# Mixture-of-experts units of 32 token slots on four column quarters of the array, with a deeper pipeline

## The chip, the cores and the metric

The kernel runs on one core of a Trainium2 chip. The metric is the device time of one execution in microseconds (us), taken as the median of several runs. A core has TensorE (PE, with PEld for its weight loads), VectorE (DVE), ScalarE (ACT), GpSimd (POOL) and SyncE (SP), 16 DMA engines that all queues share, SBUF of 128 partitions, and PSUM in 8 banks of 128 x 512 floats. Everything here is float32 unless said otherwise.

## What is computed

The reference is two layers of a hybrid trunk over 1024 tokens of width 1024. Each layer is a mixer (stick-breaking attention in layer 0, a convolution module in layer 1) followed by a mixture of experts, and the change touches only the latter:

```
idx, wts = route(hf, w_router, b_router)          # 2 of 16 experts for each token
xb = h_pad[row_tok].reshape(n_blk, EXPERT_BLOCK, D)
def expert_block(args):
    xe, e = args
    return (jax.nn.silu(xe @ w_gate[e]) * (xe @ w_up[e])) @ w_down[e]
...
y = jnp.zeros((T + 1, D), yb.dtype).at[row_tok].add(yb * row_w[:, None].astype(yb.dtype))
```

With D = 1024 and an inner width of 512, an expert has 1024 x 512 weights for gate, as many for up, and 512 x 1024 for down: 2 MB each, 6 MB in all, so 96 MB for a layer. The 2048 (token, expert) pairs of a layer fall unevenly on the experts. For the inputs of the reference the counts are 92, 109, 113, 218, 178, 178, 143, 145, 60, 133, 138, 119, 128, 133, 68, 93 in the first layer and 29, 35, 36, 24, 187, 48, 108, 187, 148, 95, 369, 284, 130, 139, 75, 154 in the second.

## The kernel before

The program is written per engine, with semaphores between the engines. For each layer, `moe(l)` on each engine does the following.

**Routing.** DVE picks the two experts of each token, PE sums the counts, and DVE turns them into `bounds` (for each expert, the number of its first unit) and `dest` (the slot of each pair). A unit is 64 slots of one expert (`UNIT`, L32). An expert gets as many units as its count needs and at least one: 40 units in the first layer and 40 in the second. Two products of one-hot tables (L1377, L1378; the tables are made in L1025 to L1032) give `slot_tok` (L1036), a table with a column for each unit that tells which row of the DRAM tensor `h_rows` each partition is to fetch. With 64 slots and 128 partitions, partition p < 64 fetches the first half (512 columns) of slot p's row and partition 64 + p the second half.

**Gather (POOL, L459 to L461).** POOL copies the unit's column of the table to `idx_now`, drains, and issues an indirect DMA of 128 rows of 2 KB to `xg`. There is one `xg`. After each gather, POOL waits for the unit's output, stores it (L474, two DMAs of 64 rows x 2 KB to `expert_rows`), and then waits until the gather has landed and the stores too, before it goes on.

**Products (PE).** For a unit b, PE multiplies the turned rows `xT` with gate and up (L1417). `xT[:, c, :]` is the stationary operand: 128 rows of the contraction by 64 slots, so it fills half of the array's columns. Two products run at a time, one for each column half (`UNIT * t`), and each half makes its own half of the inner width. A part of 256 columns holds 128 of gate and 128 of up. For each part f of two, 16 products of 256 columns fill bank f. Then PE turns the first half of `ha` (L1406), turns the next unit's gathered rows (L1386, four transposes), does the first quarter of down (L1399), turns the second half of `ha`, and does the rest of down. Down for a unit is 8 products of 512 columns, again on two column halves.

**Between them.** ACT applies silu to each part (L644) and scales half of the next unit's turned rows (L634, four activations of 128 x 64). DVE multiplies silu with up (L1064), scales the other half (L1053), copies the turned `ha` (L1069) and multiplies the unit's output by the modulation gate (L1073, 128 x 512).

**Weights (SP, L316 to L326).** Two sets of three 2 MB buffers hold the weights of an even and of an odd expert. When the last unit of expert i has done gate and up, SP issues the gate and up weights of expert i + 2 (L323), and when its down is done, the down weights (L326).

**After the units.** For each tile of 128 tokens POOL gathers the two expert rows of each token (L483), and DVE adds them to `xq` with the router's weights (L1078, L1080).

The order of the work around the change is written out by hand. Each engine has a loop over the units (or over experts and their units, on PE), and the semaphores count units.

## Time and profile before

| | |
|---|---|
| median of 3 runs | 2388.29 us (2388.24 to 2390.66) |
| the profiled execution, its own time | 2393.53 us |
| span of the profiled execution | 2391.9 us |
| granted TensorE clock, mean | 0.946 of 2.4 GHz |
| PE busy | 2167.1 us, 91% of the span |
| DVE, ACT, POOL busy | 48%, 31%, 11% |
| DMA | 391.49 MB, mean 164 GB/s |
| gate and up products (L1417) | 5120 matmul instructions, 571.9 us busy |
| down products (L1399) | 1280 matmul instructions, 311.3 us busy |

The profile is one execution of the program. A float32 product is two matmul instructions in it, a transpose is one. Busy time of PE includes its pipelining, so the distance from one start to the next tells more than the duration of one instruction. "issue" as a cause of idle time means that nothing that the profile shows was waited for. For a DMA the time to landing is from its issue to the last of its 16 semaphore updates.

### The profile page before, as it was taken

Reading aid. Unit: us, or ns where it says so; the run is one execution under the profiler, and the core shown is the slowest. Engines: PE = TensorE matmul, PEld = TensorE weight load, DVE = VectorE, ACT = ScalarE, POOL = GpSimd, SP = SyncE. Lnnn points to the kernel's source line nnn. Section 1 sums busy time; section 2 is a strip of 40 time slices with the busy share of each in tenths; the row PEclk is TensorE's granted clock in tenths of the full one; section 3 lists DMA queues with packets and bytes.
Section 4 is the critical chain, followed back from the end, with each engine's and each line's share of the span. In section 5 each row is a group of like instructions: output and inputs, shape, how many; then the busy total and the mean of one; then the engine's idle time right before and its main releaser. Section 6 shows DMA issues by size and latency. Waiting matters only on the chain.

```text
span 2391.9 us, 33087 instructions
## 1 busy us (share of the span) xinstructions
PE 2167.1 (91%) x12218; PEld 1202.3 (50%) x12219; DVE 1155.4 (48%) x2059; ACT 743.6 (31%) x1571; POOL 273.3 (11%) x465
## 2 busy tenths in 40 slices
PE   6999999999999399999998599989984899999991
PEld 2444444456666355555554367655443455555551
DVE  2355500678997622222222699999845122222225
ACT  3111100567775222222222411026252222222222
POOL 0000010000000112111112300000000111112113
PEclk8999999899999699999999699999986999999996
DMA  9166410003301665566666400300025777624646
GB/s 390 72 246 246 176 54 0 36 19 150 150 10 52 266 247 187 222 256 254 254 254 254 158 36 35 140 36 1 0 97 202 310 322 286 261 86 154 246 153 224
DMA packets 51578, 391.49 MB, mean 164 GB/s; under 512 B 9009, under 2 KB 9265, under 8 KB 33841
## 3 DMA queue, kind: packets, MB, share of 16 engines
q1 hardware_dynamic: 22514, 298.12, 30.9%
q0 software_dynamic: 28992, 92.40, 11.4%
q8 instruction: 46, 0.75, 0.1%
q14 instruction: 26, 0.21, 0.0%
HBM read 340.12 MB, written 50.37 MB: 163 GB/s over the span
## 4 chain that ended last, share of the span: by engine, by line
PE 77%; DVE 13%; DMA 5%; issue 2%; ACT 2%; POOL 0%; POOLq 0%; SPq 0%; DVEq 0%
PE ps L1417 21%; PE ps L1399 12%; PE ps L1265 9%; DVE kv L1134 8%; PE ps L1513 5%; PE ps L1283 5%; PE ps L1339 4%; PE ps L1297 3%; PE ps L1310 3%; PE ps L1322 3%; PE ps L1481 3%; DMA expert_rows<-hT 3%; PE ps L1406 2%; PE ps L1386 1%; DMA hT<-h_rows,idx_now 1%
## 5 line engine op out<-in xcount | busy, mean ns | idle before, releaser
L1134 DVE SCALAR_TENSOR_TENSOR kv<-kv,cols 128x640 f32<-128x640 f32 (+1 forms) x390 | 305.1, 782 | 13.3
L1417 PE MATMUL ps<-kv,hT 128*64 128x256 f32 x2624 | 290.9, 379 | 0.9 <-DMA kv<-in_w_gate_up 0.9
L1417 PE MATMUL ps<-ring,hT 128*64 128x256 f32 x2496 | 281.0, 384 | 10.8 <-issue 5.1
L644 ACT ACTIVATE hT<-ps 128x128 f32<-128x128 f32 x160 | 44.4, 277 | 679.8 <-PE ps L1417 679.8
L1417 PEld LDWEIGHTS ps<-kv,hT 128*64 128x64 f32 x2624 | 201.3, 137 | 101.4 <-issue 26.4
L1417 PEld LDWEIGHTS ps<-ring,hT 128*64 128x64 f32 x2496 | 193.2, 139 | 110.4 <-issue 39.7
L1453 PE MATMUL ps<-hT,ring 128*128 128x320 f32 (+1 forms) x768 | 225.4, 455 | 6.3 <-ACT hT L525 6.3
L1265 PE MATMUL ps<-hT,ring 128*128 128x512 f32 x512 | 226.5, 601 | 1.6 <-ACT hT L525 1.6
L904 DVE TENSOR_TENSOR_SCAN pbuf<-hT 128x128 f32<-128x128 f32 (+7 forms) x128 | 173.3, 1354 | 47.6 <-ACT hT L576 47.3
L1453 PEld LDWEIGHTS ps<-hT,ring 128*128 128x128 f32 x768 | 147.2, 193 | 81.1 <-ACT hT L525 7.0
L1069 DVE COPY hT<-ps 128x128 f32<-128x128 f32 x160 | 46.7, 292 | 267.3 <-PE ps L1406 267.3
L1064 DVE TENSOR_TENSOR hT<-hT,ps 128x128 f32<-128x128 f32 x160 | 45.2, 283 | 265.0 <-ACT hT L644 265.0
L1265 PEld LDWEIGHTS ps<-hT,ring 128*128 128x128 f32 x512 | 98.9, 194 | 125.9 <-issue 123.1
L1399 PE MATMUL ps<-kv,hT 128*64 128x512 f32 x656 | 158.8, 603 | 0.0
L1399 PE MATMUL ps<-ring,hT 128*64 128x512 f32 x624 | 152.5, 608 | 0.0
L1073 DVE TENSOR_TENSOR hT<-ps,bcC 128x512 f32<-128x512 f32 x80 | 55.3, 692 | 196.6 <-PE ps L1399 196.6
L634 ACT ACTIVATE hT<-ps,modc 128x64 f32<-128x64 f32 x328 | 105.7, 402 | 85.2 <-PE ps L1386 85.2
L1513 PE MATMUL ps<-ring,hT 128*128 128x512 f32 x256 | 119.4, 624 | 9.7 <-DVE kv L1148 5.8
L576 ACT ACTIVATE hT<-ps 128x128 f32<-128x128 f32 (+7 forms) x128 | 84.7, 661 | 94.8 <-PE ps L1300 89.0
L1283 PE MATMUL ps<-ring,hT 128*128 128x512 f32 x256 | 110.0, 592 | 0.0
L891 DVE SCALAR_TENSOR_TENSOR pbuf<-kv,cond,pbuf 128x512 f32<-128x512 f32 x140 | 105.3, 752 | 5.0
L474 POOL DMA_DIRECT2D expert_rows<-hT x160 | 86.0, 538 | 179.7 <-DVE hT L1073 172.9
(240 smaller groups left out, 2475.5 us busy)
## 6 DMA issues: line engine op xcount, KB each, us to landing
ring<-in_w_gate_up SPq DMA_DIRECT2D x32, 2048.0 KB, 12.5
kv<-in_w_gate_up SPq DMA_DIRECT2D x32, 2048.0 KB, 13.1
kv<-in_w_ada SPq DMA_DIRECT2D x20, 2048.0 KB, 7.6
ring<-in_w_down SPq DMA_DIRECT2D x16, 2048.0 KB, 13.9
kv<-in_w_down SPq DMA_DIRECT2D x16, 2048.0 KB
expert_rows<-hT POOLq DMA_DIRECT2D x160, 128.0 KB, 2.5
expert_rows<-ring POOLq DMA_DIRECT2D x2, 8192.0 KB, 24.7
ring<-in_w_in SPq DMA_DIRECT2D x8, 2048.0 KB, 8.1
```

The costliest lines, as they stand in the source:

```text
L474: pool.dma_start(y_dram[l][ds(b * UNIT, UNIT), 512 * h:512 * h + 512], yo[UNIT * h:UNIT * h + UNIT, :]).then_inc(stored[l], 16)
L634: ins = nc.scalar.activation(xT[:, c, :], bank(4)[:, P * j + UNIT * h:P * j + UNIT * h + UNIT], ACT.Identity, bias=modc[:, 2 * l + 1, 0, c ...
L891: ins = V.scalar_tensor_tensor(ada_sum[:, u, :], vslot[u][:, 512 * c:512 * c + 512], cond[:, c:c + 1], ada_sum[:, u, :] if c else bias[:, ...
L904: V.tensor_tensor_scan(pbuf[:, u, D - w:D][:, ::-1], omega[:, u, 0:w][:, ::-1], omega[:, u, 0:w], 1.0, ALU.mult, ALU.bypass).then_inc(scan ...
L1134: ins = V.scalar_tensor_tensor(new, old, w_dw_c[:, c, k:k + 1], new, ALU.mult, ALU.add)
L1265: ins = mm(bank(qk_bank(cc) + half), ring[:, j % 3, 512 * c + P * q:512 * c + P * q + P], hT[:, c, 512 * half:512 * half + 512], start=(c ...
L1283: ins = mm(bank(qk_bank(t) + half), hT[:, c, t * P:(t + 1) * P], ring[:, (4 + half) % 3, 512 * c:512 * c + 512], start=(c == 0), stop=(c = ...
L1339: ins = mm(wo_bank(qb, half), oTs[qb % 2][:, c, :], ring[:, half, 512 * c:512 * c + 512], start=(c == 0), stop=(c == DC - 1))
L1399: ins = mm(bank(6)[UNIT * t:UNIT * t + UNIT, :], haT[:, f, j, :], wd[:, D * (2 * j + f) + 512 * t:D * (2 * j + f) + 512 * t + 512], start= ...
L1417: ins = mm(bank(f)[UNIT * t:UNIT * t + UNIT, 0:2 * P], xT[:, c, :], wset[s][t][:, 512 * c + 256 * f:512 * c + 256 * f + 256], start=(c == ...
L1453: ins = mm(bank((gates_bank, values_bank)[part](i) + b)[:, 0:w], ring[:, j % 3, 512 * k + P * (c % 4):512 * k + P * (c % 4) + P], hT[:, k, ...
L1513: ins = mm(out_bank(t, half), hT[:, c, t * P:(t + 1) * P], ring[:, (8 + half) % 3, 512 * c:512 * c + 512], start=(c == 0), stop=(c == DC - 1))
```

## The change

`UNIT` becomes 32 and an expert gets at least two units (`MINBLK`). Counted from the inputs as above, that makes 71 units in the first layer and 73 in the second. The 128 partitions now fetch four quarters (256 columns, 1 KB) of 32 slots' rows. The stationary operand is 128 rows by 32 slots, and four products run at a time, one for each column quarter of the array: gate and up of a unit are 8 x 4 products of 256 columns into one bank, down is 4 x 4 products of 256 columns. A unit needs two transposes for its rows and one for `ha`.

On PE the order of a step is now gate and up of unit b, the transposes of the rows of unit b + 1, down of unit b - 1, and the transpose of `ha` of unit b. The first unit of each expert stands ahead of the loop over the rest, because its down half belongs to the expert before. POOL only gathers: two gathers are in flight in two halves of `xg`, and POOL copies a landed one to `xs` (128 x 256), from which PE turns it. The drains are gone. The stores have gone to ACT: four DMAs of 32 rows x 1 KB for each unit (`store`), from one of two buffers of `yo_all`. Before it issues the stores of unit b + 1, ACT waits for those of unit b to have landed. The table has 96 columns instead of 50, and two small DVE steps make the number of pairs of units.

```diff
-UNIT = 64
-MAXBLK = (2 * T + E * (UNIT - 1)) // UNIT + 1
-TABLE = MAXBLK + 2
+UNIT = 32
+QUARTERS = P // UNIT
+MINBLK = 2
+MAXBLK = 2 * T // UNIT + MINBLK * (E - 2)
+TABLE = MAXBLK + 4
+QUARTER = D // QUARTERS
...
# gpsimd, moe
-                with pool.Fori(0, blocks) as b:
-                    pool.wait_ge(x_turned2[l], b + 2)
-                    gather(b + 2)
-                    pool.wait_ge(y_kept[l], b + 2)
-                    for h in range(2):
-                        pool.dma_start(y_dram[l][ds(b * UNIT, UNIT), 512 * h:512 * h + 512],
-                                       yo[UNIT * h:UNIT * h + UNIT, :]).then_inc(stored[l], 16)
-                    pool.wait_ge(x_gathered[l], 16 * b + 48)
-                    pool.wait_ge(stored[l], 32 * b + 48)
+                with pool.Fori(0, pairs) as i:
+                    for u in (1, 0):
+                        n = 2 * i + 2 - u
+                        pool.wait_ge(x_gathered[l][u], 16 * i + 32 - 16 * u)
+                        pool.wait_ge(x_turned2[l], n)
+                        nc.gpsimd.tensor_copy(idx_now[:, u:u + 1], slot_tok[:, ds(n + 2, 1)])
+                        nc.gpsimd.tensor_copy(xs, xg[u]).then_inc(x_ready[l], 1)
+                        pool.wait_ge(table_made[l], 1)
+                        pool.wait_ge(x_ready[l], n)
+                        gather(u)
+                pool.wait_ge(rows_stored[l], 1)
...
# scalar, moe
+                def store(b, half):
+                    act.wait_ge(y_kept[l], b + 2)
+                    for q in range(QUARTERS):
+                        act.dma_start(y_dram[l][ds(b * UNIT, UNIT), QUARTER * q:QUARTER * (q + 1)],
+                                      yo_all[UNIT * q:UNIT * (q + 1), ds(half * QUARTER, QUARTER)]
+                                      ).then_inc(y_stored[l], 16)
...
+                silu(0)
+                keep(1)
+                silu(1)
+                keep(2)
+                store(0, 0)
+                with act.Fori(0, blocks - 2) as b:
+                    silu(b + 2)
+                    keep(b + 3)
+                    act.wait_ge(y_stored[l], 16 * QUARTERS * b + 16 * QUARTERS)
+                    store(b + 1, (b + 1) & 1)
...
+                store(blocks - 1, (blocks + 1) & 1)
+                act.wait_ge(y_stored[l], 16 * QUARTERS * blocks)
+                nc.scalar.activation(table_ahead[:, l:l + 1], eps[:, :], ACT.Sqrt).then_inc(rows_stored[l], 1)
...
# vector, moe: the loop over the units
+                with dve.Fori(0, blocks - 3) as b:
+                    gated_half(b + 3)
+                    keep(b + 4)
+                    keep_y(b + 2, b & 1)
+                    keep_ha(b + 3)
+                    dve.wait_ge(y_stored[l], 16 * QUARTERS * b + 32 * QUARTERS)
...
# tensor, moe
+                def gate_up(b, s):
+                    pe.wait_ge(xT_kept[l], b + 1)
+                    pe.wait_ge(xT_kept2[l], b + 1)
+                    for c in range(DC):
+                        for q in range(QUARTERS):
+                            ins = mm(bank(0)[UNIT * q:UNIT * (q + 1), 0:2 * P], xT[:, c, :],
+                                     wset[s][q // 2][:, 512 * c + 256 * (q % 2):512 * c + 256 * (q % 2) + 256],
+                                     start=(c == 0), stop=(c == DC - 1), skip_group_check=True)
+                    ins.then_inc(up_done[l], 1)
...
+                    with pe.Fori(first + 1, end) as b:
+                        gate_up(b, s)
+                        pe.wait_ge(x_ready[l], b + 1)
+                        turn_rows()
+                        pe.wait_ge(w_loaded[s][2], 16 * (E // 2) * l + 16 + 16 * i)
+                        down(b - 1, s)
+                        turn_ha(b)
```

How the instructions stand, on PE in the loop over the units of an expert. Before, `ps<-ring,hT 64x256` is gate and up, `64x512` is down, and `ps<-ident,hT` are transposes:

```order
L1412 ISA [waits xT_kept20,xT_kept0]
L1417 MATMUL ps<-ring,hT 64x256 [waits w_loaded001,w_loaded000]
L1417 MATMUL ps<-ring,hT 64x256 x31
L1405 ISA
L1406 MATMUL ps<-ident,hT 128x128 [waits ha_made0]
L1383 ISA
L1386 MATMUL ps<-ident,hT 128x128 [waits x_gathered0]
L1386 MATMUL ps<-ident,hT 128x128 x3
L1399 MATMUL ps<-ring,hT 64x512 [waits y_kept0,haT_kept0,w_loaded002]
L1399 MATMUL ps<-ring,hT 64x512
L1405 REGISTER_ALU
L1406 MATMUL ps<-ident,hT 128x128 [waits ha_made0]
```

The same loop in the changed kernel (L1446 gate and up, L1438 the rows, L1460 down, L1453 `ha`):

```order
L1446 MATMUL ps<-ring,hT 32x256 [waits xT_kept20,xT_kept0]
L1446 MATMUL ps<-ring,hT 32x256 x31
L1438 MATMUL ps<-ident,hT 128x128 [waits x_ready0]
L1438 MATMUL ps<-ident,hT 128x128
L1460 MATMUL ps<-ring,hT 32x256 [waits y_kept0,haT_kept0,w_loaded02]
L1460 MATMUL ps<-ring,hT 32x256 x15
L1453 MATMUL ps<-ident,hT 128x128 [waits ha_made0]
L1481 REGISTER_ALU
L1481 COMPARE_AND_BRANCH
```

The six down products that stood behind the second transpose of `ha` are gone from there, and all of down now stands between the transposes of two different units.

On ACT, the loop over the units before (from its first branch on):

```order
L641 UNCONDITIONAL_BRANCH
L641 ISA
L644 ACT_TABLE_LOAD
L644 ACTIVATE hT<-ps 128x128 [waits up_done0]
L643 REGISTER_ALU
L644 ACTIVATE hT<-ps 128x128 [waits up_done0]
L630 REGISTER_ALU
L634 ACTIVATE hT<-ps,modc 128x64 [waits x_turned0]
L634 ACTIVATE hT<-ps,modc 128x64 x3
L641 REGISTER_ALU
L641 COMPARE_AND_BRANCH
```

And in the changed kernel (`expert_rows<-hT` are the stores):

```order
L670 UNCONDITIONAL_BRANCH
L670 ISA
L654 ACTIVATE hT<-ps 128x128 [waits up_done0]
L644 REGISTER_ALU
L647 ACTIVATE hT<-ps,modc 128x32 [waits x_turned0]
L647 ACTIVATE hT<-ps,modc 128x32 x3
L673 ISA
L659 ISA [waits y_kept0,y_stored0]
L659 REGISTER_ALU
L659 ISA
L659 DMA expert_rows<-hT 32x256
L659 ISA
```

The table load has left the loop (it stands once, ahead of it), and four DMAs with two waits have come in behind the activations; the other three DMAs follow with an `ISA` ahead of each.

## Rows read from the trace of the kernel before

**Rows 1.** The page, busy time of each engine.
```profile
PE 2167.1 (91%) x12218; PEld 1202.3 (50%) x12219; DVE 1155.4 (48%) x2059; ACT 743.6 (31%) x1571; POOL 273.3 (11%) x465
```
**Rows 2.** The page, the chain that ended last, shares by engine.
```profile
PE 77%; DVE 13%; DMA 5%; issue 2%; ACT 2%; POOL 0%; POOLq 0%; SPq 0%; DVEq 0%
```
**Rows 3.** Windows over the units of each layer: PE, PEld, DVE, ACT, POOL, clock.
```profile
833.70:1308.50 474.80, 471.48 (x3440) 264.22 (x3440) 111.82 (x359) 124.50 (x280) 90.06 (x159) 0.99 0.63 243
1860.80:2343.80 483.00, 472.30 (x3440) 263.82 (x3440) 111.94 (x359) 124.50 (x280) 90.22 (x159) 0.99 0.58 226
```
**Rows 4.** Timeline of PE over one unit: start, us, instruction, count, idle before.
```profile
1001.30 7.08 PE L1417 MATMUL ps<-kv,hT 128*64 128x256 f32 x64
1008.31 0.33 PE L1406 MATMUL ps<-ident,hT 128*128 128x128 f32 x1
1008.48 0.60 PE L1386 MATMUL ps<-ident,hT 128*128 128x128 f32 x4
1009.07 1.08 PE L1399 MATMUL ps<-kv,hT 128*64 128x512 f32 x4
1010.08 0.33 PE L1406 MATMUL ps<-ident,hT 128*128 128x128 f32 x1
1010.34 2.79 PE L1399 MATMUL ps<-kv,hT 128*64 128x512 f32 x12
1012.97 7.08 PE L1417 MATMUL ps<-kv,hT 128*64 128x256 f32 x64
```
**Rows 5.** Line L1236 (router scores on four quarters), 790 to 795: ns min/median/max, first and last start.
```profile
L1236 PE MATMUL ps<-hT,wr x64: 272/273/297, 790.9 to 792.6; 128*32 128x128 f32 x64
```
**Rows 6.** Timelines of ACT and DVE at that unit's end.
```profile
1008.42 0.28 ACT L644 ACTIVATE hT<-ps 128x128 f32<-128x128 f32 x1 [3.18 <-PE ps L1417]
1008.89 1.29 ACT L634 ACTIVATE hT<-ps,modc 128x64 f32<-128x64 f32 x4 [0.19 <-PE ps L1386]
1010.20 1.28 ACT L644 ACT_TABLE_LOAD   x1
...
1001.52 0.69 DVE L1073 TENSOR_TENSOR hT<-ps,bcC 128x512 f32<-128x512 f32 x1 [2.44 <-PE ps L1399]
...
1009.11 1.10 DVE L1053 TENSOR_SCALAR hT<-ps,modc 128x64 f32<-128x64 f32 x4
```
**Rows 7.** Timelines of SP and POOL around a load of one expert's weights.
```profile
855.58 0.93 SPq L323 DMA_DIRECT2D ring<-in_w_gate_up  x2
860.34 0.33 SPq L326 DMA_DIRECT2D ring<-in_w_down  x1
...
857.50 1.02 POOL L461 DMA_INDIRECT hT<-h_rows,idx_now  x1 [1.06 <-issue]
861.55 1.12 POOL L474 DMA_DIRECT2D expert_rows<-hT  x2 [3.04 <-DVE hT L1073]
870.94 0.18 POOL L459 COPY idx_now<-slot_tok 128x1 int32 x1 [8.27 <-DMA expert_rows<-hT]
```
**Rows 8.** Window over that load: the last two are the DMA engines' share and GB/s.
```profile
857.00:873.00 16.00, 16.00 (x114) 8.99 (x114) 4.01 (x12) 4.60 (x9) 3.10 (x5) 1.00 0.97 407
```
**Rows 9.** Landing of that gather, of its unit's stores, of stores without a load (897 to 900).
```profile
DMA to landing us min/median/max: 9.0/9.0/9.0
...
DMA to landing us min/median/max: 7.1/7.7/8.3
...
DMA to landing us min/median/max: 2.2/2.3/2.5
```
**Rows 10.** Timeline of PE, second layer: third to fifth expert, with idle before.
```profile
1886.32 7.13 PE L1417 MATMUL ps<-ring,hT 128*64 128x256 f32 x64 [0.47 <-issue]
...
1900.72 7.13 PE L1417 MATMUL ps<-kv,hT 128*64 128x256 f32 x64 [0.94 <-DMA kv<-in_w_gate_up]
...
1916.68 7.13 PE L1417 MATMUL ps<-ring,hT 128*64 128x256 f32 x64 [2.62 <-DMA ring<-in_w_gate_up]
```
**Rows 11.** Timeline of PE, first unit of the first layer.
```profile
833.73 10.00 PE L1417 MATMUL ps<-ring,hT 128*64 128x256 f32 x64 [1.56 <-DVE hT L1053]
```
**Rows 12.** Timeline of DVE, making the table.
```profile
822.14 0.98 DVE L1027 TENSOR_TENSOR hT<-lane,kv 128x800 bf16<-128x800 f32 x1
823.16 0.43 DVE L1030 TENSOR_SCALAR hT<-hT,tokid 128x800 bf16<-128x800 bf16 x1
823.51 1.05 DVE L1032 TENSOR_TENSOR hT<-hT,tile_first 128x400 bf16<-128x400 bf16 x2
```
**Rows 13.** Timeline of POOL, start of the second layer's gathers and end of the first layer.
```profile
1854.77 1.01 POOL L461 DMA_INDIRECT hT<-h_rows,idx_now  x1 [4.04 <-issue]
...
1310.29 1.12 POOL L474 DMA_DIRECT2D expert_rows<-hT  x2 [2.90 <-DVE hT L1073]
1314.24 1.00 POOL L483 DMA_INDIRECT kv<-expert_rows,dest  x1 [2.83 <-DMA expert_rows<-hT]
```

More of the change, by code:

```diff
@@ new lines, in gather @@
+                        in_offset=bass.IndirectOffsetOnAxis(ap=idx_now[:, u:u + 1], axis=0)).then_inc(x_gathered[l][u], 16)
+                for u in range(2):
+                    nc.gpsimd.tensor_copy(idx_now[:, u:u + 1], slot_tok[:, u:u + 1]).then_inc(idx_made[l], 1)
+                    pool.wait_ge(idx_made[l], u + 2)
+                    gather(u)
+                pairs = pool.value_load(bounds[0:1, E + 1:E + 2], min_val=1, max_val=(MAXBLK + 1) // 2)
+                pool.wait_ge(x_gathered[l][0], 16)
@@ L637, in keep @@
-                    ins.then_inc(xT_kept[l], 1)
-                keep(0)
-                blocks = act.value_load(bounds[0:1, E:E + 1], min_val=1, max_val=MAXBLK)
-                with act.Fori(0, blocks) as b:
-                    for f in range(2):
-                        act.wait_ge(up_done[l], 2 * b + f + 1)
-                        nc.scalar.activation(sg[:, P * f:P * f + P], bank(f)[:, 0:P], ACT.Silu).then_inc(silu_done[l], 1)
-                    keep(b + 1)
+                    for q in range(QUARTERS):
+                        c = 2 * q
+                        ins = nc.scalar.activation(xT[:, c, :], bank(4)[:, UNIT * q:UNIT * (q + 1)],
+                                                   ACT.Identity, bias=modc[:, 2 * l + 1, 0, c:c + 1],
+                                                   scale=modc[:, 2 * l + 1, 1, c:c + 1])
@@ new lines, in keep, with silu @@
+                    ins.then_inc(xT_kept[l], 1)
+                def silu(b):
+                    act.wait_ge(up_done[l], b + 1)
+                    nc.scalar.activation(sg, bank(0)[:, 0:P], ACT.Silu).then_inc(silu_done[l], 1)
+                def store(b, half):
+                    act.wait_ge(y_kept[l], b + 2)
+                    for q in range(QUARTERS):
+                        act.dma_start(y_dram[l][ds(b * UNIT, UNIT), QUARTER * q:QUARTER * (q + 1)],
+                                      yo_all[UNIT * q:UNIT * (q + 1), ds(half * QUARTER, QUARTER)]
+                                      ).then_inc(y_stored[l], 16)
@@ new lines, in moe @@
+                keep(0)
+                dve.wait_ge(gate_loaded, 80 * (l + 1))
+                blocks = dve.value_load(bounds[0:1, E:E + 1], min_val=MINBLK * E, max_val=MAXBLK)
+                gated_half(0)
+                keep(1)
+                keep_ha(0)
+                for b in (1, 2):
+                    gated_half(b)
+                    keep(b + 1)
+                    keep_y(b - 1, (b + 1) % 2)
+                    keep_ha(b)
+                dve.wait_ge(y_stored[l], 16 * QUARTERS)
@@ new lines, in turn_ha, with down @@
+                def turn_ha(b):
+                    pe.wait_ge(ha_made[l], b + 1)
+                    nc.tensor.transpose(bank(2)[:, 0:P], ha, ident[:, :]).then_inc(ha_turned[l], 1)
+                def down(b, s):
+                    pe.wait_ge(haT_kept[l], b + 1)
+                    pe.wait_ge(y_kept[l], b + 1)
+                    for f in range(QUARTERS):
+                        for q in range(QUARTERS):
+                            ins = mm(bank(6)[UNIT * q:UNIT * (q + 1), 0:QUARTER], haT[:, UNIT * f:UNIT * (f + 1)],
+                                     wset[s][2][:, D * f + QUARTER * q:D * f + QUARTER * (q + 1)],
+                                     start=(f == 0), stop=(f == QUARTERS - 1), skip_group_check=True)
+                    ins.then_inc(down_done[l], 1)
@@ new lines, in expert @@
+                def expert(i, s, very_first=False):
+                    first = pe.value_load(bounds[0:1, ds(2 * i + s, 1)], min_val=0, max_val=MAXBLK)
+                    end = pe.value_load(bounds[0:1, ds(2 * i + s + 1, 1)], min_val=MINBLK, max_val=MAXBLK)
+                    for k in range(2):
+                        pe.wait_ge(w_loaded[s][k], 16 * (E // 2) * l + 16 + 16 * i)
+                    if very_first:
+                        gate_up(0, s)
+                        pe.wait_ge(x_ready[l], 1)
+                        turn_rows()
+                        turn_ha(0)
+                    else:
+                        gate_up(first, s)
+                        pe.wait_ge(x_ready[l], first + 1)
+                        turn_rows()
+                        down(first - 1, 1 - s)
+                        turn_ha(first)
+                    with pe.Fori(first + 1, end) as b:
+                        gate_up(b, s)
+                        pe.wait_ge(x_ready[l], b + 1)
+                        turn_rows()
+                        pe.wait_ge(w_loaded[s][2], 16 * (E // 2) * l + 16 + 16 * i)
+                        down(b - 1, s)
+                        turn_ha(b)
@@ L1433, in _ @@
+                pe.wait_ge(idx_made[l], 4)
+                turn_rows()
+                expert(0, 0, very_first=True)
+                expert(0, 1)
+                with pe.Fori(1, E // 2) as i:
+                    for s in range(2):
+                        expert(i, s)
+                last = pe.value_load(bounds[0:1, E:E + 1], min_val=MINBLK * E, max_val=MAXBLK)
+                down(last - 1, 1)
             for t in range(TT - 2):
```

197 lines of the change are left out of this document (78 added, 119 removed).

## The prediction

> **What bounds the kernel now.** I read four views. First the page: PE is busy for 91% of the span, more than twice as much as DVE, the next engine [rows 1], and the chain that ended last runs over PE for 77% [rows 2]. Then the windows over the units: the two layers' units take 474.8 + 483.0 = 957.8 us of the 2391.9, and in both PE leaves only 3 and 11 us idle while DVE and ACT are busy for a quarter of the time [rows 3]. All that the change touches in earnest lies in these windows. Third, the timeline of PE over one unit: from one unit's first product to the next one's it is 11.67 us, with no gap anywhere [rows 4]. So a unit costs what PE needs for it, and 80 units (40 and 40) explain 80 x 11.67 = 933.6 of the 957.8 us. Last, the DMA rows: a load of one expert's 6 MB occupies the queues for some 16 us at a 0.97 share [rows 8], and everything issued meanwhile lands late [rows 9]. Behind PE that costs little now; the reader should keep it in mind.
>
> **The step of 32 slots on PE.** Per slot nothing is saved in the products; what is saved is padding. The units go from 80 of 64 slots (5120) to 71 + 73 = 144 of 32 (4608), 10% less. The cost of a unit comes out of one timeline [rows 4]. From the first product of gate and up to the first transpose it is 7.01 us for 16 pairs, from down's first product to the next transpose 1.01 us for one pair of twice the width. Both fit 0.427 us for 256 columns and 0.16 to 0.18 us for each change to or from transposes. Four transposes take 0.59 us, one takes 0.26, so two 0.37. The new unit:
> - gate and up, 8 groups of four: 8 x 0.427 + 0.18 = 3.59
> - two transposes of rows: 0.37
> - down, 4 groups of four: 4 x 0.427 + 0.16 = 1.87
> - one transpose of `ha`: 0.26
>
> That is 6.09 us, and 144 x 6.09 = 877 us.
>
> This rests on four quarters really running together. The trace has that case: the router's scores put 32 products of 128 columns on four quarters, and their 64 instructions start within 1.7 us [rows 5], 0.21 us for each group of four, just half of the 0.427 for half the width. The new gate and up issue 64 instructions in 3.4 us, so at half that pace.
>
> What the windows hold besides (24 us now) stays nearly: the step from one pass over two experts to the next, 0.5 us some 15 times, 8 us; the lower clock of the first unit, whose gate and up take 10.0 instead of 7.08 us [rows 11], 4 us over both layers; the wait for weights in the second layer. There the first four experts have one unit each, now two. Their compute goes from 11.7 to 12.2 us each, both under the 16 us of a load, so the fifth expert starts where it does, at 1916.7 [rows 10]; that is 55.8 us after the first, and 55.8 - 4 x 12.2 = 7 us of waits remain. New is the end: down of the last unit cannot overlap another gate and up, 2.3 us a layer, 4.6. Sum: 877 + 8 + 4 + 7 + 4.6 = 901 us, against 957.8: **57 us less**.
>
> **Gathers.** POOL now spends a copy of 0.18 us and an issue of 1.0 us [rows 7], and the new copy of 128 x 256, which I put at 0.3 to 1 us (DVE takes 0.69 for 128 x 512 [rows 6]; POOL at half that rate is my upper end). At most 3 us in each 6.1, so covered. A gather is issued some 15 us before its transposes; the slow one took 9.0 us [rows 9]. Covered too, and if it weren't, PE would wait at the first transpose. Without the drain, which holds the second layer's first gather for 4.04 us [rows 13], that layer starts 3 us sooner.
>
> **The table.** 96 columns instead of 50: the four operations took 0.98 + 0.43 + 1.05 us for 50 [rows 12], so about 2.2 us more, plus two small steps of 0.2. On the path, twice: +5 us.
>
> **The end of a layer.** Stores to first expert-row gather is 3.95 us now [rows 13]. ACT issues four DMAs instead of two; SP's issues of this kind are 0.59 us apart (two end 0.93 after the first began, one takes 0.33 [rows 7]). So the last goes out 1.8 us after the first and lands 2.2 later [rows 9], 4.0, and a square root with its table load (1.28 [rows 6]) stands behind: +1.5 us a layer, +3.
>
> So far: -57 - 3 + 5 + 3 = **-52 us**.
>
> **The stores on ACT, the term that decides.** Put 0 at the end of a unit's gate and up stream. Silu starts at 0.3 and the four activations end by 2.0 [rows 4, 6]. Down ends at 0.18 + 0.37 + 1.71 = 2.26, DVE's product for 128 x 256 takes about 0.43 (0.69 for 512 columns [rows 6]) and starts 0.3 after, so ACT can issue its stores at 3.2. Four at 0.59 are done at 5.5, the branch at 5.7; the next silu is due at 6.4. The table load of 1.28 us that closed each unit [rows 6] is no longer in the loop; with it, ACT would be late every time. So 0.7 us are spare on ACT, and PE still has 0.4 before it needs `xT`: **1.1 us** in all.
>
> Behind the wait for the last unit's stores, ACT has its next stores and then the next silu queued, and DVE and PE follow that. If the stores take L us to land, ACT can issue no more often than every L us. Without a load L is 2.2 + 1.8 = 4.0, under 6.09: nothing. Within a load, the trace has one related case [rows 7, 9]: the gather landed at 857.50 + 9.0 = 866.5, the second of the two stores queued behind it at 862.1 + 8.3 = 870.4. Two transfers thus took 3.9 us. The same rows in four transfers: at best 3.9 plus the 1.8 us of issuing, 5.7; at worst each costs 1.95 us as before and the first still needs its 2.2, 10.0. I take 7.0, nearer the lower end, since each transfer has half as many rows. A load of 16 us takes in two such stores. They come 0.9 + 0.9 us late, less 1.1 spare: 0.7 us for each of the 28 loads that run beside units, **+20 us**. At L = 5.7 it is 0; at 8.3 the first is 2.2 late and the second, which the end of the load helps, 0.9: 2.0 each, +56; at 10 about 4.3 each, +120.
>
> Sum: -52 + 20 = -32 us. The profiled execution took 2393.5 us (span 2391.9), 5.2 above the median of 2388.3; against the median that is **2356 us**, 1.3% less.
>
> **Rivals.**
> *Stores land within the period.* L is 6.4 or less and ACT is never late: 2388.3 - 52 = 2336 us. For it: without a load they land in 2.2 to 2.5 us [rows 9]. Against it: 7 to 8 us for two within one.
>
> *Stores late, slower than before.* The place is ACT's wait for landed stores. From L = 8.1 or so each load costs over 1.9 us, 28 loads eat the 52, and the kernel is slower. At L = 9: 2.9 + 1.2 - 1.1 = 3.0 us x 28 = 84, 2420 us. For it: each small transfer has an end of its own to be waited for, four instead of two, and POOL's gathers are in flight beside. Against it: half the rows in each, and a queue that no gather stands ahead in. The Trainium skill (DMA: Bandwidth & Descriptors, Queues, rings and completion order) says that each DMA engine goes round its queues packet by packet, so a short transfer waits for a weight packet at every turn. By that rule the number of turns counts, not bytes, which speaks for this rival; rows 9 agree as far as they go.
>
> *A wait I don't see.* The step is 0.3 us longer than 6.09, from four semaphores a unit or DVE's order (scaling, then the output product): 144 x 0.3 = 43 us, 2399 us. Against it: none of these waits shows in the present unit [rows 4].
>
> *The instructions don't come fast enough.* If they came only at the present pace, 64 in 6.83 us, gate and up and down would take twice as long and the kernel over 3000 us. Rows 5 speak against it: 27 ns per instruction, where 53 are needed. The Trainium skill (TensorE: Matmul & The Clock Gate, the section on the gap of 56 ns) knows a decoding in software at about 62 ns for each matmul instruction. By that figure a unit would be some 0.8 us longer, an estimate of 120 us more. The pace in rows 5 is quicker than that rule allows, so it hardly counts here.
>
> **How the numbers follow.** Forecast (stalls of 8 to 45 us, 2344 to 2381): 0.50. Stores hidden: 0.18. Stores late: 0.22. Unseen wait: 0.07. Instruction pace: 0.03. A measurement of this kernel can tell 0.2% (4.8 us) from no change. Faster by more than that: 0.68. Of the rest 0.06 fall within it, where the late stores just eat the gain, and 0.26 are slower. The range reaches from 4 us below the hidden case (a small sum of my roundings) to the middle of the late case: 2332 to 2415 us; what lies beyond is under 0.2.
>
> **What would show it.** PE's distance from unit to unit should be 6.1 us outside loads. The router's stage should grow by 2 to 3 us. Silu's idle time should end with gate and up; where ACT's stores wait for `expert_rows` and PE's products then wait for `xT`, within loads alone, that is the +20. The forecast is wrong if the distance outside loads is over 6.3, or if the stores in a load take over 8 us or under 6 us.

## The result and the profile after

The changed kernel takes 2516.97 us in the median of its runs (2509.2 to 2524.0), the kernel before 2388.26 in the same session. The ratio is 1.0537, with a 95% interval of 1.0515 to 1.0558: **5.4% slower** where I had forecast 1.3% faster. It lies outside the range too, on the side of the rival *stores late, slower than before*, and 97 us above the time which I gave that rival.

The page of the changed kernel, against [rows 1, 2]: busy time, and the chain that ended last by engine and by line.
```profile
PE 2167.3 (86%) x19590; PEld 1192.4 (47%) x19591; DVE 1188.7 (47%) x2351; ACT 699.0 (28%) x1735; POOL 316.2 (13%) x595
...
PE 62%; DVE 14%; DMA 13%; ACTq 4%; issue 4%; ACT 2%; POOL 0%; DVEq 0%; SPq 0%; POOLq 0%
PE ps L1446 15%; DMA expert_rows<-hT 12%; PE ps L1319 9%; DVE kv L1188 7%; PE ps L1460 6%; PE ps L1579 5%; PE ps L1337 4%; PE ps L1393 4%; ACTq L659 4%; PE ps L1351 3%; PE ps L1364 3%; PE ps L1376 3%; PE ps L1547 2%; PE ps L1438 1%; PE ps L
```
PE is busy for the same 2167 us, but its share fell from 91 to 86%. What is new in the chain is a transfer, the stores of the experts' rows: 12% of it is their landing and 4% their issue on ACT. A store has no reader before the end of a layer, so a chain that runs over it runs over a wait for its buffer.

The windows over the units of both layers, against [rows 3] (busy time of PE, PEld, DVE, ACT, POOL; then granted clock, DMA share, GB/s):
```profile
833.40:1367.90 534.50, 464.48 (x7029) 255.97 (x7029) 125.23 (x496) 100.90 (x356) 107.57 (x214) 0.93 0.55 212
...
1921.20:2474.40 553.20, 479.44 (x7227) 260.28 (x7227) 128.60 (x510) 103.63 (x366) 110.54 (x220) 0.93 0.52 194
```
The units now take 534.5 + 553.2 = 1087.7 us, 130 more than before, and that is the whole loss: the stretch between the layers takes 553.3 us, before 552.3. PE idles for 70 and 74 us instead of 3 and 11, and the granted clock was 0.93 instead of 0.99.

The timeline around one load of weights shows how (start, us, engine, line, operation, count, idle time before and what ended it). L1446 is gate and up, L1460 down, L1453 the transpose of `ha`, L654 silu, L659 the stores.
```profile
853.36 1.96 ACTq L659 DMA_DIRECT2D expert_rows<-hT  x4
856.35 0.44 PE L1438 MATMUL ps<-ident,hT 128*128 128x128 f32 x2
856.47 0.28 ACT L654 ACTIVATE hT<-ps 128x128 f32<-128x128 f32 x1 [4.87 <-PE ps L1446]
...
858.84 3.66 PE L1446 MATMUL ps<-kv,hT 128*32 128x256 f32 x64
...
862.43 0.44 PE L1438 MATMUL ps<-ident,hT 128*128 128x128 f32 x2
862.80 1.93 PE L1460 MATMUL ps<-kv,hT 128*32 128x256 f32 x32
...
866.47 2.68 ACTq L659 DMA_DIRECT2D expert_rows<-hT  x4
869.48 0.28 ACT L654 ACTIVATE hT<-ps 128x128 f32<-128x128 f32 x1 [11.58 <-DMA expert_rows<-hT]
...
870.14 0.48 PE L1453 MATMUL ps<-ident,hT 128*128 128x128 f32 x1 [5.41 <-DVE hT L1098]
...
871.11 5.20 PE L1446 MATMUL ps<-kv,hT 128*32 128x256 f32 x64 [0.49 <-DVE hT L1091]
...
878.73 3.66 PE L1446 MATMUL ps<-kv,hT 128*32 128x256 f32 x64
```
The stores issued from 853.36 us hold ACT until they have landed, 12.8 us later; the next four go out at 866.47 and take 2.68 us to issue; only then comes the silu that was due at 862.6. It is 6.9 us late, and DVE and PE follow. Behind the stall gate and up take 5.20 instead of 3.66 us. The windows over the gate and up ahead of the stall and behind it (the granted clock is the figure before the last two) show why:
```profile
858.84:862.43 3.59, 3.59 (x65) 1.98 (x65) 0.62 (x2) 0.00 (x0) 0.40 (x1) 1.00 1.00 417
871.11:876.30 5.19, 5.19 (x65) 2.79 (x66) 0.38 (x2) 0.00 (x0) 0.00 (x0) 0.69 0.10 25
```
PE had been idle for 5.9 us but for one transpose, and the granted clock behind that is 0.69 instead of 1.00. The distance from 858.84 to 871.11 is 12.27 instead of 6.08 us, the next one 7.62.

The waits between the start and the end of the units, in total, times, longest:
```profile
ACT hT L654 <- DMA expert_rows<-hT: 189.8, 21, 12.0
ACT hT L654 <- issue: 161.7, 18, 10.7
...
PE ps L1453 <- DVE hT L1098: 102.8, 34, 5.8
```
ACT's waits in these rows are not all losses, since ACT is idle in every step. PE's are: 34 waits of some 3 us for the product behind a late silu.

Over all units (from the starts of L1446 in groups of 64 in the trace) the distances add up to 199.5 us above 6.083 each, and 56.9 us of these are gate and up that took longer than usual.

### The profile page after: what moved, and what is told of

Read it like the earlier page. It is cut to its first block, busy times and chain, and to the rows that moved or that the text cites. A ratio compares the mean times of both kernels' runs of the same rounds, so it can differ in the third digit from the quotient of the medians.

```text
span 2521.3 us, 51133 instructions
## 1 busy us (share of the span) xinstructions
PE 2167.3 (86%) x19590; PEld 1192.4 (47%) x19591; DVE 1188.7 (47%) x2351; ACT 699.0 (28%) x1735; POOL 316.2 (13%) x595
## 4 chain that ended last, share of the span: by engine, by line
PE 62%; DVE 14%; DMA 13%; ACTq 4%; issue 4%; ACT 2%; POOL 0%; DVEq 0%; SPq 0%; POOLq 0%
PE ps L1446 15%; DMA expert_rows<-hT 12%; PE ps L1319 9%; DVE kv L1188 7%; PE ps L1460 6%; PE ps L1579 5%; PE ps L1337 4%; PE ps L1393 4%; ACTq L659 4%; PE ps L1351 3%; PE ps L1364 3%; PE ps L1376 3%; PE ps L1547 2%; PE ps L1438 1%; PE ps L1266 1%
## 5 line engine op out<-in xcount | busy, mean ns | idle before, releaser
L1446 PE MATMUL ps<-ring,hT 128*32 128x256 f32 x4544 | 291.3, 413 | 27.8 <-issue 15.4
L1446 PE MATMUL ps<-kv,hT 128*32 128x256 f32 x4672 | 292.8, 407 | 13.8 <-DVE hT L1091 7.1
L654 ACT ACTIVATE hT<-ps 128x128 f32<-128x128 f32 x144 | 40.0, 278 | 875.0 <-PE ps L1446 523.5
L1446 PEld LDWEIGHTS ps<-ring,hT 128*32 128x32 f32 x4544 | 166.6, 119 | 130.4 <-issue 48.6
L1446 PEld LDWEIGHTS ps<-kv,hT 128*32 128x32 f32 x4672 | 164.8, 117 | 118.4 <-issue 32.0
L647 ACT ACTIVATE hT<-ps,modc 128x32 f32<-128x32 f32 x584 | 173.2, 379 | 67.6 <-PE ps L1438 67.6
L467 POOL DMA_INDIRECT hT<-h_rows,idx_now x152 | 148.3, 976 | 116.9 <-POOL hT L487 108.7
L1091 DVE TENSOR_SCALAR hT<-ps,modc 128x32 f32<-128x32 f32 x584 | 140.5, 303 | 9.6 <-PE ps L1438 9.6
L1460 PE MATMUL ps<-kv,hT 128*32 128x256 f32 x2336 | 142.9, 385 | 1.8 <-DVE hT L1102 1.8
L1453 PE MATMUL ps<-ident,hT 128*128 128x128 f32 x144 | 49.7, 345 | 102.9 <-DVE hT L1098 102.8
L1460 PE MATMUL ps<-ring,hT 128*32 128x256 f32 x2272 | 137.3, 382 | 0.0
L1579 PE MATMUL ps<-ring,hT 128*128 128x512 f32 x256 | 117.0, 614 | 9.7 <-DVE kv L1202 5.8
L486 POOL COPY idx_now<-slot_tok 128x1 int32 x146 | 27.1, 185 | 743.3 <-PE ps L1438 743.3
L1106 DVE TENSOR_TENSOR hT<-ps,bcC 128x256 f32 (+1 forms) x144 | 60.9, 423 | 121.9 <-PE ps L1460 116.9
## 6 DMA issues: line engine op xcount, KB each, us to landing
kv<-in_w_down SPq DMA_DIRECT2D x16, 2048.0 KB, 10.1
```

Source lines behind the costliest of these rows:

```text
L467: pool.indirect_dma_start(out=xg[u], out_offset=None, in_=h_dram[l].rearrange("t (q d) -> (t q) d", q=QUARTERS), in_offset=bass.IndirectOf ...
L647: ins = nc.scalar.activation(xT[:, c, :], bank(4)[:, UNIT * q:UNIT * (q + 1)], ACT.Identity, bias=modc[:, 2 * l + 1, 0, c:c + 1], scale=mo ...
L1091: ins = V.tensor_scalar(xT[:, c, :], bank(5)[:, UNIT * q:UNIT * (q + 1)], modc[:, 2 * l + 1, 1, c:c + 1], modc[:, 2 * l + 1, 0, c:c + 1], ...
L1446: ins = mm(bank(0)[UNIT * q:UNIT * (q + 1), 0:2 * P], xT[:, c, :], wset[s][q // 2][:, 512 * c + 256 * (q % 2):512 * c + 256 * (q % 2) + 25 ...
L1460: ins = mm(bank(6)[UNIT * q:UNIT * (q + 1), 0:QUARTER], haT[:, UNIT * f:UNIT * (f + 1)], wset[s][2][:, D * f + QUARTER * q:D * f + QUARTER ...
L1579: ins = mm(out_bank(t, half), hT[:, c, t * P:(t + 1) * P], ring[:, (8 + half) % 3, 512 * c:512 * c + 512], start=(c == 0), stop=(c == DC - 1))
```

## The experiments

Three theories at first. **W**: it is ACT's wait for landed stores, in front of silu, that costs. **D**: a transfer that lands late holds the unit whoever waits for it. **P**: the new pipeline is slow by itself. "Excess" is the sum of the distances above 6.083 us. "Landing in a load" is the mean time from the first issue of a unit's stores to the last landing (from semaphore events in the trace), over those that took more than 9 us; in the two runs where nearly all are shorter, over 6.5.

**Stores from POOL.**
```diff
-act.wait_ge(y_stored[l], ...); store(b + 1, (b + 1) & 1)        # in ACT's loop
+pool.wait_ge(y_stored[l], 16 * QUARTERS * (n - 2)); store(n - 2, u)   # in POOL's, behind gather(u)
```


> Theory W (ACT's wait for the last unit's stores, with the next silu queued behind it, holds PE during a load of weights): with the four stores issued and waited for by POOL, ACT is free. The stores still land in 8 to 12 us during a load, but POOL has some 4 us of spare time before the next copy to xs is late, so the time falls to 2340 to 2390 us. Rival D (the late landing itself, by DVE's wait for a free output buffer or by the DMA queues, holds the units whoever waits): 2450 us or more.

Measured: 2591.4 us, ratio 1.0851 (1.0826 to 1.0876), slower still. Taken by the letter, that speaks for D. But the waits say who was late now:
```profile
POOL expert_rows L486 <- DMA expert_rows<-hT: 187.9, 36, 6.9
...
PE ps L1449 <- POOL hT L495: 166.5, 112, 5.4
```
L495 is POOL's copy of the gathered rows to `xs`, L1449 their transposes. POOL, too, has work that PE needs behind the wait. Four issues of 2.3 us also made its step longer than PE's: 126 of 142 distances are over 6.3 us, outside loads as well. So the run moved the wait to a fuller queue and did not take it away; it doesn't tell W from D.

**Fewer transfers.** Two transfers of 64 rows of 1 KB, and one of 128, for four of 32. They write the rows in another order, so the output is permuted.
```diff
-for q in range(QUARTERS): act.dma_start(y_dram...[32 rows, quarter q], yo_all[UNIT * q:UNIT * (q + 1), ...])
+for q in range(n): act.dma_start(y_dram...[UNIT // n rows].rearrange("t (q d) -> (t q) d", q=4), yo_all[P // n * q:P // n * (q + 1), ...])
```


> As one store, but two DMAs of 64 rows x 1 KB. If the number of transfers sets the landing, it lies about half way: 7 to 9 us and 2370 to 2440 us. If rows or a fixed delay set it, as with one store.

> The unit's output goes out in one DMA of 128 rows x 1 KB instead of four of 32 rows, to a place in expert_rows that makes the DRAM side contiguous (the layout is then not the one that the combination reads, so the output differs). Same bytes, same wait on ACT. If the number of transfers sets the landing during a load (each end of a transfer waits behind a weight packet), it falls from 12 to about 5 or 6 us and the kernel to 2340 to 2380 us. If the rows or bytes set it, or a fixed delay behind the weights already queued, the landing stays over 9 us and the kernel over 2440 us.

Measured, one run each: 2479.1 us with two, 2430.8 with one, against 2517 with four (whose four runs lie up to 15 us apart). Excess 199.5, 141.0 and 98.0 us; landing in a load 11.2, 10.9 and 10.1 us. Most of a landing remains: even one transfer, which lands in 1.8 us without a load, takes 10 within one. The 1.1 us that fewer transfers save within a load are no more than they save without one (3.0 to 1.8 us). The larger gain is on ACT, which issues the next stores before the late silu. With one transfer that takes 0.70 us, where it took 3.01 above (866.47 to 869.48):
```profile
865.91 0.35 ACTq L660 DMA_DIRECT2D expert_rows<-hT  x1
866.61 0.28 ACT L654 ACTIVATE hT<-ps 128x128 f32<-128x128 f32 x1 [7.29 <-issue]
```

One thing must be taken off the times of all runs whose first layer comes out wrong: the second layer then routes its tokens otherwise. The silus of the second layer, one for each unit, in the changed kernel, with no loads (below), and with two units' stores in flight as four transfers and as one (below):
```profile
L654 ACT ACTIVATE hT<-ps x73: 277/278/278, 1927.1 to 2469.2; 128x128 f32<-128x128 f32 x73
L654 ACT ACTIVATE hT<-ps x75: 277/277/278, 1849.0 to 2307.3; 128x128 f32<-128x128 f32 x75
L654 ACT ACTIVATE hT<-ps x74: 277/277/278, 1847.8 to 2309.2; 128x128 f32<-128x128 f32 x74
L654 ACT ACTIVATE hT<-ps x76: 277/277/278, 1845.8 to 2316.9; 128x128 f32<-128x128 f32 x76
```
The runs with one transfer, with two, with no loads and with half the packets (below) all have 75 units there instead of 73. Two units are 12.2 us, so that two transfers and one compare as 2467 and 2419 us with the 2517. The excess isn't touched by it.

**No loads.** The loads in the loops move 64 of 4096 columns of the weights, so the experts compute with wrong ones.
```diff
-sp.dma_start(wset[s][k], w_gate_up[...])
+sp.dma_start(wset[s][k][:, 0:64], w_gate_up[...][:, 0:64])      # also for w_down
```


> The loads of weights that run beside the units move 64 of 4096 columns, so the products of all but the first two experts use stale weights; everything else, all waits too, is as in the changed kernel. Theory W and D: no load, no late landing, so 2388 - 52 (the sum without the term of the stores) - 7 (no wait for weights) = 2329, within 2320 to 2345 us. Rival P (the new pipeline is slower by itself, by ACT, DVE or the instruction pace): over 2400 us.

Measured, one run: 2361.6 us, excess 20.9. P is out: without traffic the distance is 6.08 us nearly everywhere. It came 33 us above the 2329 of my sum and 17 above my upper end. Of the 33, 12.2 are the two units more; some 7 are the last silu of the first layer, late beside the convolution's loads; some 12 are what the steps between experts cost, which I had put too low (below).

**Two units' stores in flight.** This takes away what makes ACT wait: four output buffers instead of two, one semaphore for the even and one for the odd units, and ACT waits for the stores of two units before (the count of the odd ones starts at 16). DVE's waits for landed stores go too. They asked for nothing more than ACT's: in the changed kernel the product that stands behind DVE's wait needs a silu that stands behind ACT's wait for the same stores.
```diff
-with act.Fori(0, blocks - 2) as b:
-    silu(b + 2); keep(b + 3); act.wait_ge(y_stored[l], 64 * b + 64); store(b + 1, (b + 1) & 1)
+with act.Fori(1, pairs - 1) as i:
+    silu(2 * i + 2); keep(2 * i + 3); act.wait_ge(odd[l], 64 * i + 16);   store(2 * i + 1, 1)
+    silu(2 * i + 3); keep(2 * i + 4); act.wait_ge(even[l], 64 * i + 64);  store(2 * i + 2, 0)
+# DVE without waits for landed stores; buffer b & 3; the last expert gets a unit more where the number is odd
```


> The four stores of a unit stay on ACT, but ACT waits for those of two units before instead of one: a semaphore for the even and one for the odd units, four output buffers instead of two, and the number of units made even (one more unit in each layer, which costs 2 x 6.1 = 12 us at most). Theory W (it is ACT's wait for landed stores that costs): a landing of 10 to 13 us is then covered by two steps of 6.08 (12.2 us), or by one stretched step and one more; of the 199.5 us that the distances of the change lie above 6.08 us, all but some 20 to 40 go, and the time is 2350 to 2385 us. Theory D (whoever waits, a store or gather that lands late holds the unit): 2450 us or more. A third, Q (the queue is bound by what it can carry in a load, so that a second unit in it lands only later): the landings of stores in a load grow from 10 to 13 us to 18 or more, and the time is 2430 to 2500 us.

Measured: **2362.7 us, ratio 0.9899 (0.9883 to 0.9914)**, 1.0% faster than the kernel before and 6% faster than the change, though it runs two units more. The timeline of ACT in its first load:
```profile
855.81 1.96 ACTq L659 DMA_DIRECT2D expert_rows<-hT  x4
859.26 0.28 ACT L654 ACTIVATE hT<-ps 128x128 f32<-128x128 f32 x1 [4.86 <-PE ps L1460]
...
862.43 2.37 ACTq L659 DMA_DIRECT2D expert_rows<-hT  x4
865.36 0.28 ACT L654 ACTIVATE hT<-ps 128x128 f32<-128x128 f32 x1 [4.67 <-PE ps L1460]
...
869.17 3.02 ACTq L659 DMA_DIRECT2D expert_rows<-hT  x4
872.24 0.28 ACT L654 ACTIVATE hT<-ps 128x128 f32<-128x128 f32 x1 [5.46 <-DMA expert_rows<-hT]
```
Stores land no sooner (11.4 us in a load, 13.0 for the first), but silu follows gate and up. Only the third silu shown is late, by 0.8 us behind stores that waited for those of 855.81; that is within the 1.1 us of spare time, and PE's next gate and up starts within 0.1 us of its time. Its windows:
```profile
836.40:1287.90 451.50, 441.17 (x7128) 245.95 (x7128) 128.49 (x503) 102.39 (x361) 107.56 (x214) 1.00 0.66 251
1841.90:2314.30 472.40, 456.59 (x7326) 250.42 (x7326) 132.37 (x517) 105.52 (x371) 110.52 (x220) 0.99 0.59 228
```
The excess is 30.3 us, and the clock is back at 1.00 and 0.99. W holds, D and Q fall: stores that land as late as before cost next to nothing once ACT doesn't wait for them. Of the 30.3 us, 20.9 stood there without loads too, and some 7 belong to the fourth expert of the second layer, whose weights came late and whose first gate and up was slow (distances of 10.4 and 8.8 us):
```profile
1885.01 6.42 PE L1460 MATMUL ps<-kv,hT 128*32 128x256 f32 x64 [4.28 <-DMA kv<-in_w_gate_up]
```

> As the run with two units' stores in flight, but one transfer of 128 rows of 1 KB for a unit instead of four of 32. W: the landing of one transfer was already short enough that with two in flight nothing of it is left to wait for; 2340 to 2370 us, within 15 us of the run with four. D: as the run with one transfer and one in flight, 2430 us or more. Q: between the two, 2390 to 2430 us, and a large distance from the run with four transfers in flight. Under W this beats the kernel before (2386 to 2388 us).

Measured (the output permuted as with one transfer above): 2371.5 us, ratio 0.9939 (0.9925 to 0.9952). It is 9 us slower than with four, and has 76 units in the second layer where that has 74, 12.2 us. For the same units it would be 3 us faster, and its excess is 27.1 us, 3 less. With two in flight, one transfer instead of four buys next to nothing, as W says.

**What sets the landing.** Over the first landing in a load of the changed kernel, and over its first 3.5 us apart (queue, kind: packets, MB, share of the 16 engines; q1 carries the loads, q0 the gathers, q10 ACT's stores):
```profile
q1 hardware_dynamic: 338, 5.01, 92.5%
q0 software_dynamic: 96, 0.26, 5.1%
q10 hardware_dynamic: 192, 0.13, 3.2%
...
q1 hardware_dynamic: 87, 1.43, 97.1%
q0 software_dynamic: 13, 0.05, 3.7%
```
In the 3.5 us after the issue not one packet of a store moved. Without a load the first one moved 0.8 us after the issue. Behind that, 128 packets of 1 KB and 64 that signal, 12 on each engine, went out among some 250 of the loads. That is some 16 weight packets on each engine beside 12 of the stores. Two theories: **N**, the number of packets counts, since each takes turns with a weight packet of 16 KB; **F**, a store that meets a load waits for its end.

```diff
-for q in range(QUARTERS): act.dma_start(...)      # 128 packets
+for q in range(2): act.dma_start(...)             # 64 packets, half the rows' columns left zero
```


> The change with two stores for a unit, of the first two quarters (32 rows of 1 KB each); the other two quarters of the experts' rows stay zero (the zeros ahead are written to all rows, some us of DMA time in the attention stage). So two transfers as in the run with two stores, with half its packets: 64 of 1 KB instead of 128, 4 on each of 16 engines instead of 8. Theory N (number of packets: within a load a store's packet and a weight packet of 16 KB, 0.61 us, take turns on each engine, so that a landing is about 4 us ahead of the first packet and 0.6 us for each packet behind it): the first landing within a load falls from the 10.5 to 12 us of the run with two stores by 4 x 0.61 = 2.4 us to 8 to 9.5 us, and the time from 2479 to 2395 to 2440 us. Theory F (a store that meets a load waits for its end, however few its packets are): the landing stays at 10 to 12 us and the time at 2465 to 2495 us.

```diff
-sp.dma_start(wset[s][k], src)
+for c in range(2): sp.dma_start(wset[s][k][:, 2048 * c:2048 * (c + 1)], src[:, 2048 * c:2048 * (c + 1)])
```


> The change, with each weight load of 2 MB issued as two transfers of 1 MB (columns 0 to 2047 and 2048 to 4095), so that a weight packet has 8 KB instead of 16 KB; the bytes are the same. N: a weight packet takes some 0.31 us instead of 0.61, and so does each turn that a store's or a gather's packet waits; the first landing in a load falls from 10.4 to 13.2 us to 7 to 9 us, and the time from 2517 to 2400 to 2450 us. F: landings and the time stay, 2500 to 2530 us. If transfers of 8 KB packets carry fewer bytes a second, loads end later, and some of the gain is lost: up to 2480 us.

Measured: with half the packets 2411.4 us, ratio 1.0105 (1.0085 to 1.0125), landing in a load 8.0 us (in the first layer 8.0 to 9.5 for the first of a load) and excess 75 us; with weight packets of 8 KB 2439.5 us, ratio 1.0213 (1.019 to 1.0237), landing 8.1 us and excess 116.5 us. Both are where N puts them, F is out. (The first of these times has the two units more in it, the second has not.) What shrank are the turns: the first packet of a store still came 3.5 us after the issue in both runs. The profile does not tell the engine of a packet, so that they alternate one by one is inferred from these counts and times. During such a landing of the second run its loads moved at this rate:
```profile
q1 hardware_dynamic: 496, 3.61, 90.5%
```
That is 3.61 MB in 9.6 us, 376 GB/s, against 5.01 in 12.8, 391, with packets of 16 KB. In these two stretches the smaller packets cost the loads 4% of their rate, and they took over a quarter off the mean landing.

**One gather in flight**, on the version with two units' stores in flight.
```diff
-idx_now[u] <- slot_tok[n + 2]; copy xs; gather(u)
+idx_now[1 - u] <- slot_tok[n + 1]; copy xs; gather(1 - u)
```


> The version with two units' stores in flight, with one gather in flight instead of two: POOL gathers the rows of the next unit behind the copy of this one, not those of the one after. A gather then has one step (6.1 us less the copy) to land. Outside loads it lands in some 2.3 us and nothing changes. Within a load it took 9.0 us in the kernel before, and 10 to 12 us with the change; each of the 28 loads then holds one to three units by 4 to 6 us, with the low clock behind it: 2362.7 + 28 x 6 to 28 x 10 gives 2520 to 2650 us. Rival: the next rows are needed a whole unit later than they are copied, so that the second gather in flight is worth nothing: 2360 to 2385 us.

Measured: 2390.7 us, ratio 1.0023 (1.0009 to 1.0037), 28 us more than with two.
```profile
POOL idx_now L483 <- DMA hT<-h_rows,idx_now: 475.4, 105, 8.1
```
POOL waits for its gather at 105 of 146 units, up to 8.1 us, but the excess rises only from 30.3 to 57.3 us. The rows are copied to `xs` when the transposes before have freed it, and PE asks for them a step later: most of the landing was covered without the second gather. My main expectation was wrong by over 100 us, the rival nearly right. The second gather is worth 28 us.

**Down behind its own gate and up**, on the same version.
```diff
-gate_up(b, s); turn_rows(); down(b - 1, s); turn_ha(b)
+gate_up(b, s); turn_rows(); turn_ha(b); down(b, s)
```


> The version with two units' stores in flight, with the products down of a unit behind its own gate and up, not behind those of the next. From its trace (a unit at 911.69 to 917.77 us): down then waits for silu (0.28), the product (0.29), the transpose (0.33), DVE's modulated rows ahead in its order (0.96) and the copy (0.28), with the handovers some 2 us of which the transposes of rows cover 0.4. A step becomes 7.4 to 7.6 us instead of 6.08, so 144 x 1.4 = +200 us: 2540 to 2590 us if the work one unit ahead is what makes 32 rows pay. Rival: the steps are held by the copies of rows or by ACT, and PE would have waited anyway: 2365 to 2400 us.

Measured: 2573.4 us, ratio 1.0774 (1.0756 to 1.0792). Its timeline:
```profile
1002.07 3.66 PE L1460 MATMUL ps<-ring,hT 128*32 128x256 f32 x64
1005.67 0.44 PE L1452 MATMUL ps<-ident,hT 128*128 128x128 f32 x2
...
1006.45 0.33 PE L1467 MATMUL ps<-ident,hT 128*128 128x128 f32 x1 [0.34 <-DVE hT L1114]
...
1007.90 1.93 PE L1474 MATMUL ps<-ring,hT 128*32 128x256 f32 x32 [1.12 <-DVE hT L1118]
1009.62 3.66 PE L1460 MATMUL ps<-ring,hT 128*32 128x256 f32 x64
```
A step is 7.55 us: PE waits 0.34 us for the product and 1.12 for the copy of the transpose. Working one unit ahead is worth 211 us here; without it the units of 32 would be slower than the kernel before.

**Both cures together.** Two units' stores in flight and weight packets of 8 KB, by the two edits above.

> The version with two units' stores in flight, with weight loads as two transfers of 1 MB each (packets of 8 KB). If nothing that lands late in a load holds a unit any more, the shorter landings buy nothing: within 0.2% of 2362.7 us. If the last stretched units (30 us above 6.08 us, most of it at the ends of the first layer's and in the first experts of the second) come from landings, 2345 to 2357 us. If 8 KB packets make loads longer, 2367 to 2380 us.

Measured: 2359.4 us, ratio 0.9881 (0.9865 to 0.9898), excess 28.4 us. The first answer, within 0.2%: the landings in a load fell from 11.1 to 8.5 us (means over those of more than 6.5 us), and that bought nothing that these runs can tell, once no one waits for them.

## Why the prediction was wrong

**The step of 6.09 us: right.** The distances outside loads are 6.08 us. The quarters run together, and none of the waits I feared is in a step: with no loads most distances are 6.08 us too.

**Boundaries: sized at less than half.** I put 0.5 us at some 15 steps, 8 us. Without stalls the version in flight shows 0.9 us at the step from one pair of experts to the next and 0.3 within one (distances of 7.0 and 6.4 us), some 20 us with those at the start of a layer's loop. The windows of the version in flight, 923.9 us, less two units (12.2), are 911.7 against my 901. My 7 us of waits for weights are right in size: 4.3 us of wait, and 2.8 in a gate and up that took 6.42 us behind it.

**Gathers, table, end of a layer: small, as said.** The copy to `xs` takes 0.39 us, within my bounds. The first unit starts at 833.4 us against 833.7 before, at 836.4 in the version in flight; between the layers 553.3 against 552.3.

**ACT's schedule: right.** Four issues take 1.9 us, stores without a load land 3.0 us after the first issue (I had 4.0), and the table load is gone. The 1.1 us of spare time covered the silu that was 0.8 us late.

**The landing in a load: the step that failed.** It is the sentence "Two transfers thus took 3.9 us", the source of the term L. It takes the landing of the gather (866.5) as the moment from which the stores were served, and subtracts the time which they had waited until then. But ACT waits from the issue, and [rows 9] have that time: 8.3 us for the second store, 7.1 at the least. The part that I subtracted is no wait for the gather ahead that a free queue would save. In the changed kernel nothing of a store moved for 3.5 us or so after most issues into a load, with no gather in its queue. The next sentences then scaled a part, 5.7 to 10.0, where the whole was asked for, and "I take 7.0" leant to the lower end "since each transfer has half as many rows": the runs show that the number of packets and the turns which they wait count, and these are 128 packets of 1 KB whether in four transfers or in one. Measured: 11.2 us in the mean over 33 landings, 13.2 at most; the mean is above even my upper end, 10.0.

"A load of 16 us takes in two such stores" was wrong as well, to the other side: with ACT held by the first, the next came as the load ended (5.45 us for the one issued at 866.47). 35 landings took more than 6.5 us, for 28 loads.

The formula behind it was nearly right. With the measured landings, L - 6.09 adds up to 170.6 us over those 35. Less 1.1 us of spare time for each that is 132 us, where I had 20.

**The clock: in the sum for the first units alone (4 us).** PE idles for some 5 us in such a stall, and the gate and up behind it took 5.2 us instead of 3.66 at a granted clock of 0.69. Over all units this item is 56.9 us; in the version without stalls it is 6.5, so the stalls brought some 50. The distances hold 132 + 57 + some 20 for the boundaries, 209 us, where 199.5 were measured: the parts overlap a little, or the formula is some 10 us high.

**The rival.** *Stores late* had the place, the mechanism and the rule of turns from the Trainium skill (DMA: Bandwidth & Descriptors, Queues, rings and completion order), which the packet counts and the runs with half the packets and with weight packets of half the size bear out as far as they go. It had 0.22, and a price at L = 9. "A queue that no gather stands ahead in", which I held against it, did not help: the queue had no gather ahead, and its stores took 11.2 us. The price, 84 us at L = 9, lacked the clock.

**What each part is worth**, around the version in flight (2362.7 us): working a unit ahead 211 us, the second gather 28 us, and stores that ACT need not wait for 154 us (2517.0 to 2362.7, with two more units of 12.2 us in it). The change had the first two and lacked the third.

## What to carry to other kernels

Price a wait for a landing from issue to landing, as the waiting engine sees it, in the stretch where the queues are full, and compare that with the period of the loop; when a change halves the period, every wait that was covered must be priced anew. Where it doesn't fit, put one more transfer in flight (a buffer and a semaphore) before making it smaller. Look at what stands behind a wait in its engine's queue: moved from ACT to POOL, the same wait held PE through other work. And when an experiment makes wrong values, count the units of work again before comparing times: what the first layer gets wrong can change how much the second has to do.

## What the runs showed of the hardware

- A store of 1 KB rows issued into running loads moved no packet for some 3.5 us, against 0.8 without a load, and weight packets of 8 KB instead of 16 left that as it was. With its 128 packets among those of the loads, 128 KB took 10 to 13 us as a rule instead of 1.8 to 3.0. Half the packets made it 8.0 us, weight packets of half the size 8.1.
- More transfers for the same 128 packets cost about as much within a load (10.1, 10.9 and 11.2 us for one, two and four) as without one (1.8, 2.7 and 3.0).
- Small issues can stretch too: four on ACT took 1.96, 2.37, 2.68 and 3.02 us within a load, 1.87 without.
- Behind 5.9 us in which PE was idle but for one transpose the granted clock was 0.69 over the next gate and up, which took 5.20 instead of 3.66 us.
- The second store in flight does not slow the first: 11.2 us with one unit's stores in flight, 11.4 with two.
